# Fourteen slots instead of eighteen in the ring of expert weight chunks

## The reference: what is computed

```
probs = softmax(h @ router_w)                       # 16 experts
gate, idx = top_k(probs over the tokens, cap)       # cap 64 latent + 16 context tokens for each expert
xs  = h[idx]
hid = silu(xs @ wg[e]) * (xs @ wu[e])               # 1024 -> 2048, two matrices
ye  = hid @ wd[e] * gate                            # 2048 -> 1024
f   = scatter-add of ye over the tokens
```

## Time and profile before

| | us |
|---|---|
| median of 3 runs (lowest, highest) | 1556.12 (1554.01, 1557.94) |
| the profiled execution, its own time | 1558.57 |
| its span, first instruction to last | 1556.3 |
| PE busy in the span | 1386.4 (89%) |
| DVE, ACT, POOL busy | 681.1, 269.8, 125.3 |
| bytes moved by DMA | 479.81 MB |

### The profile page before, as it was taken

One profiled execution on the slowest core, in us unless ns is written; L12 is line 12 of the kernel. 1 busy time (PEld: TensorE's weight loads), 2 busy tenths in 40 slices (PEclk: granted clock), 3 DMA queues, 4 the chain that ended last, 5 costly groups with the idle time before them and its releaser, 6 DMA issues.

```text
span 1556.3 us, 25121 instructions
## 1 busy us (share of the span) xinstructions
PE 1386.4 (89%) x11009; PEld 574.5 (37%) x11009; DVE 681.1 (44%) x1219; ACT 269.8 (17%) x448; POOL 125.3 (8%) x81
## 2 busy tenths in 40 slices
PE   5699889676991899999999999999999999999990
PEld 1587667553860222222222222222223333333330
DVE  1536554342256425354362454443634534345333
ACT  2224335220240001101111011010111110111102
POOL 0422331020000000000000000000000000000000
PEclk9699999887985899999999999999999999999995
DMA  9421110457449899999999999999999999999964
GB/s 361 146 82 55 54 54 26 137 182 270 149 169 331 294 394 395 412 398 397 414 397 397 412 397 414 393 394 412 395 394 413 392 412 391 392 412 391 406 254 143
DMA packets 124274, 479.81 MB, mean 308 GB/s; under 512 B 11534, under 2 KB 13834, under 8 KB 107788
## 3 DMA queue, kind: packets, MB, share of 16 engines
q1 hardware_dynamic: 113796, 453.55, 74.6%
q0 software_dynamic: 3072, 10.49, 2.8%
q10 hardware_dynamic: 7304, 14.23, 2.5%
HBM read 464.59 MB, written 13.64 MB: 307 GB/s over the span
## 4 chain that ended last, share of the span: by engine, by line
PE 74%; DMA 11%; DVE 9%; ACT 3%; issue 2%; ACTq 0%; POOL 0%; SPq 0%; POOLq 0%; DVEq 0%
PE bank L1025 25%; PE bank L1042 13%; PE bank L1030 13%; PE bank L1047 6%; DMA late<-in_exp_up 4%; PE bank L353 3%; PE bank L354 3%; PE bank L355 3%; DMA raw<-in_ada_w 3%; DMA arena<-in_exp_up 1%; PE bank L736 1%; DMA raw<-in_exp_up 1%; PE bank L786 1%; DVE arena L1225 1%; PE bank L868 1%
## 5 line engine op out<-in xcount | busy, mean ns | idle before, releaser
L1025 PE MATMUL bank<-late,xs_t 128*32 128x512 f32 x1200 | 287.5, 599 | 27.1 <-DVE xs_t L1430 14.8
L1027 PE MATMUL bank<-late,xs_t 128*32 128x512 f32 x1200 | 286.4, 599 | 0.0
L1461 DVE SCALAR_TENSOR_TENSOR arena<-bank,gate,arena 64x512 f32<-64x512 f32 x64 | 73.1, 1142 | 296.8 <-ACT arena L678 294.6
L1413 DVE STREAM_TRANSPOSE arena<-arena 32x256 f32<-32x256 f32 x372 | 161.9, 435 | 72.4 <-PE bank L1047 66.6
L678 ACT ACTIVATE arena<-bank 64x512 f32<-64x512 f32 x64 | 37.7, 589 | 802.5 <-PE bank L1030 801.7
L1030 PE MATMUL bank<-late,xs_t 128*16 128x512 f32 x1200 | 157.6, 596 | 0.0
L1025 PEld LDWEIGHTS bank<-late,xs_t 128*32 128x32 f32 x1200 | 73.0, 111 | 213.9 <-issue 190.9
L1413 DVE STREAM_TRANSPOSE xs_t<-arena 32x256 f32<-32x256 f32 x204 | 88.8, 435 | 111.5 <-DMA arena<-xn_rows,slot_tok 108.5
L1025 PE MATMUL bank<-arena,xs_t 128*32 128x512 f32 x496 | 119.0, 599 | 2.1 <-DMA arena<-in_exp_up 2.0
L1027 PE MATMUL bank<-arena,xs_t 128*32 128x512 f32 x496 | 118.5, 600 | 0.0
L1042 PE MATMUL bank<-late,arena 128*32 128x512 f32 x992 | 118.0, 592 | 0.0
(11 more groups left out here) (226 smaller groups left out, 1748.6 us busy)
## 6 DMA issues: line engine op xcount, KB each, us to landing
late<-in_exp_gate SPq DMA_DIRECT2D x75, 1024.0 KB, 20.7
late<-in_exp_up SPq DMA_DIRECT2D x75, 1024.0 KB, 19.3
late<-in_exp_down SPq DMA_DIRECT2D x66, 1024.0 KB, 20.3
raw<-in_exp_down SPq DMA_DIRECT2D x40, 1024.0 KB, 19.4
arena<-in_exp_gate SPq DMA_DIRECT2D x31, 1024.0 KB, 21.7
arena<-in_exp_up SPq DMA_DIRECT2D x31, 1024.0 KB, 20.9
raw<-in_ada_w SPq DMA_DIRECT2D x24, 1024.0 KB, 8.9
raw<-in_exp_gate SPq DMA_DIRECT2D x22, 1024.0 KB, 22.8
```

Source lines behind the costliest of these rows:

```text
L1025: mm(psum[b][32 * i:32 * i + 32, :], lat[i], g[:, j, c], start=first, stop=final)
L1027: mm(psum[b][64 + 32 * i:96 + 32 * i, :], lat[i], u[:, j, c], start=first, stop=final)
L1413: last = nc.vector.transpose(dst[:, :, 0:32], src[s0:s0 + 32, :].rearrange("p (k f) -> p k f", k=KT)[:, :, q:q + 32])
L1461: stt(hid_out(0, CAP_L, b), rows4(psum[b][64:128, :]), gate[64:128, p:p + 1], rows4(sgl[64:128, b, :]), ALU.mult, ALU.mult)
```

## The change

One constant: the ring has 14 slots. The ring's list of buffers, its semaphores, the slot of a chunk (g modulo RING) and SP's wait (`x_used` at least g - RING + 1) all follow from it. The tile `arena` no longer receives chunks; its size and the other uses of it stay. Chunks 14 to 17, which were issued without a wait on PE, now wait for chunks 0 to 3 to be used, and each later chunk waits for a use that lies four chunks later than before.

```diff
-RAW, LATE, RING, WS = 4, 10, 18, 3
+RAW, LATE, RING, WS = 4, 10, 14, 3
```

## The result

Fourteen slots: 1565.83 us, median of 6 runs (1562.2 to 1568.19), against 1553.92 us (1549.33 to 1557.94) for eighteen in 6 runs of the same comparison. The ratio is 1.0072 with a 95% interval of 1.0051 to 1.0094, so 8 to 15 us slower, 11.2 at the ratio; the forecast was 1566.4 us.

A forecast was written before the change was run, and what follows sets the result against it. Transfers were taken to bound the expert stage, 64.9 us an expert against PE's 61.8. Profiled 1558.57 + 10.3 (four chunks) = 1568.9 us; against the three-run median of 1556.12, 1566.4 us; range 1560 to 1572 us.

The forecast's parts named there:

- Who waits for whom: Expert stage: transfers need 64.9 us an expert, 3.1 us more than PE, which lives on chunks landed before it began.
- what had landed when the engines ran dry at 534 us: At 534 us 22 chunks have landed, not 26; saturated engines then stay four chunks behind to the end.
- Four times a chunk's time: Last landing in the chain comes later by four chunks' transfer time, taken as 10.3 us.
- The bounds of 10.1 to 10.8 us: Four chunks' time: 10.1 us at the fastest slice's 414 GB/s, 10.8 us with a gather's and scatter's share in each.
- No pinch at fourteen: Saturated stretch: fourteen slots come round in 37.9 us against 30 us held, so fewer slots cost zero; pinch rival's chance 0.05.
- Where PE runs out: PE's first wait for weights moves from 1223 to about 1020 us (990 to 1040); such waits grow from 10.4 to about 20.
- the chain turns to landings: Sign of being right: the chain turns to landings of up chunks at about 1020 us in place of 1209.
- ten experts: Before the change, PE lives for ten experts on chunks landed before it began, running out at about 1223 us.
- The shorter queue that serves the transfers cheaper: Rival, 538 us to the end: gathers and scatter-adds cost less; saving 0.74 us an expert gives 1556 us; chance 0.07.
- The clock's dip behind the last wait: Rival: PE's clock falls behind the last wait, some 30 us before PE's end, adding 1.7 us: 1568.1 us; chance 0.08.
- the change does nothing: Rival: end waits were hiccups around scatters with PE the bound on average, so 1556 us; chance 0.05.

## Why the prediction was right

**Who waits for whom.** The transfers are the slower side by 3.1 us an expert, and PE lives on a lead. Shown: the pace of 64.9 us stayed to the tenth; with PE made the slower side no cost of the change can be told.

**The price is a number of chunks, not the late start of four loads.** The forecast tied the loss to what had landed when the engines ran dry at 534 us. Shown by holding back the four loads with the slots kept: 2.6 us in place of 11.2. The trace's DMA records show it as a count as well. Between 34 and 36 us after PE's first expert matmul nothing lands on SP's queue in the kernels with eighteen, sixteen, fourteen, ten and eight slots and no held loads, and up to there it had landed 72.0 MB (of 2^20 bytes, the prologue's among them) with eighteen, 70.0 with sixteen, 68.0 with fourteen, 64.0 with ten and 62.0 with eight: one chunk less for each slot given up.

**Four times a chunk's time.** 10.3 us was forecast; 11.2 us by the ratio (8 to 15), 10.9 us in the profile from PE's start to the last wanted landing, 5.0 us for half the change. The bounds of 10.1 to 10.8 us were a little narrow for a single profile. From nineteen slots down to ten a slot costs 2.4 to 3.1 us by the ratios, 2.57 within each interval. That the time met the forecast to 0.6 us is in part luck: the median of eighteen slots came out 2.2 us lower than the 1556.12 that the sum began with, and the difference of the medians, 11.9 us, 1.6 us higher than forecast.

**No pinch at fourteen.** Costed at zero with the queue's waiting time as cover, and shown: eight slots still keep the engines at 402 GB/s in the window from 1000 us.

**Where PE runs out.** Forecast 990 to 1040 us, measured 980, so a miss by some 10 us; the chain turns to landings at 1032.86 + 27.82 = 1060.7 us, where 1020 was said. A reading that fits: PE's waits come at a few places of an expert, so the first wait moves by whole experts, 10.3 / 3.1 = 3.3 rounds up to four, 4 x 61.8 = 247 us, and 1225.8 - 980.05 = 245.7 us it was. It is not a rule: from fourteen to ten slots the first wait moved to 785.4 us, by 194.7 us or 3.2 experts. The prediction's "ten experts" before PE runs out are 11.7 of its own 61.8 us, from 502 to 1223 us; nothing in its sum rests on them.

**The rivals.** The shorter queue that serves the transfers cheaper is out: with issue to landing down by 7 us the rate is the same. The clock's dip behind the last wait did not come: that wait was 0.9 us, the granted clock from 1492 to 1500 us is 1.00, and behind 1492 us the tail took 1563.2 - 1492.0 = 71.2 us, 72.0 before. That the change does nothing is out by the interval.

**Open.** Eight slots lose 3.5 us less than their count, ten 1.6 less. For ten that lies within the interval of the ratio (16.6 to 21.5 us against 20.6); for eight, 18.8 to 25.5 us, the count of 25.7 lies just outside. Measured in the profiles from PE's first expert matmul to the end of the span, the losses are 22.4 us with ten slots and 23.8 with eight. PE started its experts at 497.23 us with ten and at 496.70 with eight, against 502.12 with eighteen; but it started at 497.16 with sixteen too, although the same chunks are issued up to there as with eighteen. The first gather does not separate them either: from issue to landing it took 8.2 us with eighteen, 7.4 with fourteen, 5.8 with sixteen and 5.6 with ten and with eight. So the prologue varies by some 5 us between profiles whatever the ring, and whether a small ring shortens it was not separated.

## What to carry to other kernels

Where loads and compute run at nearly the same pace, find out from two places of the chain which is slower, by how much for each round, and when its engines were last without work; behind that moment a slot of prefetch is worth about one slot's transfer time as long as the ring still keeps the transfers saturated, and nothing that could be told here if the compute is the slower side. How deep a ring must be to keep the transfers saturated is a different and much smaller number (eight here), and below it the loss grows steeply. A buffer that idles for most of a kernel, like the row of gains, may be worth more as a slot. What to check first is how many landings are behind when the engines last stand idle: that number, and not the length of the idle time, was the price.

## What was not expected of the hardware

The rate of the transfers did not depend on the queue's length over a wide range: from 1000 to 1130 us it was 402 GB/s with a median issue-to-landing time of 21.6 us and of 14.7 us. With seven slots and 12.0 us it was 403 GB/s there, but 396 over the whole stretch from 560 to 1450 us. It fell to 367 GB/s at 10.8 us and to 309 GB/s at 9.6 us. From eight slots of 1 MB to six the loss goes from 22 to 109 us, and with five it is 296.

With a long queue the issue of a load was itself slow: a median of 4.3 and 3.3 us for the gate chunks above, 0.37 us with eight slots. Four slots more or less changed nothing in the issue-to-landing time, 21.8 us in both kernels.
